# Expert weights moved as whole matrices, 16 KB in a row per partition, and activations turned by VectorE

## The chip, the cores and the metric

The kernel runs on one core of a Trainium2 chip. The metric is the device time of one launch in microseconds; the kernel before was timed in three runs.

## The reference

The program is a two-layer trunk on 256 tokens of 1024 numbers, all in float32. Layer 0 mixes tokens by causal pooling, layer 1 by differential attention; behind each mixer stands a mixture of 32 experts, of which every token uses two. The part that matters here is the expert block:

```
def expert_block(args):
    xb, e = args
    a = jax.nn.silu(xb @ w1[e]) * (xb @ w3[e])
    return a @ w2[e]
```

`w1` and `w3` are 1024x512 and `w2` is 512x1024, 2 MB each, so one expert is 6.3 MB of weights and the two layers together are 403 MB. About 16 tokens choose an expert on average.

## The kernel before

Nearly all that is read from memory are expert weights. They pass through `ring`, eight slots of 16 KB per partition (2 MB each). One slot holds one *chunk*, and an expert is three chunks (`CPE = 3`). Chunk 0 is the first half of the input rows of w1 and w3 together, chunk 1 the second half of both, chunk 2 is w2. SyncE issues every chunk as two transfers of 1 MB. In chunks 0 and 1 each partition gets 8 KB in a row from each matrix; in chunk 2 a partition reads four separate rows of w2, 4 KB each.

SyncE issues a chunk when its slot has been read: chunk `c` takes the slot of chunk `c-8`, and `used` says on what it waits. Slots with a first-half chunk come free at the semaphore `half`, those of a second-half chunk at `gu`, those of w2 at `y`. The eight first chunks of a layer are loaded ahead, in layer 1 behind the attention weights that stood in the slots.

TensorE works through the experts in groups of four (`E4`). For one expert (`expert(k)`) it does in this order: `gate_up` on chunk 0 and on chunk 1 (h times w1 and w3, 32 tokens a block, four column tiles of 32 side by side), `gather` of a quarter of the next group's tokens, a transpose of the activations `act`, and `down` on chunk 2. ScalarE and VectorE make silu(gate) * up between `gate_up` and the transpose, and VectorE copies the turned activations `actT` back from PSUM. After four experts `scatter` adds the results to their tokens. A second block of 32 tokens is skipped by a branch where an expert has at most 32 tokens.

```
used = (main["half"], main["gu"], main["y"])
...
sp.wait_ge(used[j], it * BODY + (layer * NE + e + 1))
load(c % RING, chunk_parts(layer, it * BODY + c // CPE, c % CPE), loaded[c % RING])
```

Of the kernel before, what the change touches and what calls it, by code (L numbers as in the profile page):

```python
# [18 lines left out]
ALU = mybir.AluOpType  # L19
ACT = mybir.ActivationFunctionType  # L20
# [73 lines left out]
def build(nc, x, norm_mix_g, norm_ffn_g, pool_w, pool_scale, wq, wk, wv, wo, lq1, lk1, lq2, lk2, subln_g,  # L94
          moe_wg, moe_bg, moe_we, moe_be, moe_w1, moe_w3, moe_w2, final_g, consts, out):
    with ExitStack() as ctx:
# [69 lines left out]
        at_ps = ps[:, 7, 0:256].rearrange("p (b r) -> p b r", b=NB)  # L166
# [39 lines left out]
        STEPS = ("onehot", "gated", "xg", "xgc", "half", "gu", "exp", "den", "sig", "gh", "act", "at", "atc", "y", "yc_v", "yc_a",  # L206
# [12 lines left out]
        def chunk_parts(layer, e, j):  # L219

            if j < 2:
                return [(m * 2048, w[layer, e, :, :].rearrange("(p k) n -> p k n", k=KT)[:, 4 * j:4 * j + 4, :])
                        for m, w in ((0, moe_w1), (1, moe_w3))]
            w = moe_w2[layer, e, :, :].rearrange("(j p) n -> p j n", p=P)
            return [(m * 2048, w[:, 2 * m:2 * m + 2, :]) for m in range(2)]

        def attn_parts(c):
            w = (wv, wq, wk, wo)[c // 2]
            if c < 6:
                w = w[0].rearrange("(p k) n -> p k n", k=KT)  # L230
            else:
                w = w[0].rearrange("(k p) n -> p k n", p=P)
            at = 4 * (c % 2)
            return [(m * 2048, w[:, at + 2 * m:at + 2 * m + 2, :]) for m in range(2)]

        def view(src):
            return src.shape[1], src.shape[2]
# [5 lines left out]
        def _(sp):  # L243
            def load(slot, parts, signal):
                for at, src in parts:
                    k, n = view(src)
                    sp.dma_start(ring[:, slot, at:at + k * n].rearrange("p (k n) -> p k n", k=k), src) \  # L247
                      .then_inc(signal, 16)
# [18 lines left out]
            used = (main["half"], main["gu"], main["y"])  # L267
# [65 lines left out]
        def _(pe):  # L333
# [72 lines left out]
            def group(s, g, u, placed, rounds, fullest, tokens, chunk):  # L406
# [9 lines left out]
                def expert(k):  # L416
# [4 lines left out]
                    for half in range(2):  # L421
                        w = ring[:, chunk(k, half), :].rearrange("p (m k n) -> p m k n", m=2, k=4)

                        def gate_up(b, qs, half=half, w=w):
                            for q in qs:
                                for j in range(JT):
                                    mm = pe.matmul(gu_ps[SB * j:SB * (j + 1), b, :, :], xg[:, u, 4 * half + q, b, k, :],  # L427
# [791 lines left out]
```

## Time and profile before

| | us |
|---|---|
| median of three runs (lowest, highest) | 1174.48 (1172.45, 1177.19) |
| the profiled execution's own time | 1172.21 |
| its span in the trace | 1170.4 |
| TensorE busy, VectorE busy, ScalarE busy | 888.4, 352.2, 216.5 |
| time of DMA packets of SyncE's queue, share of 16 engines' span | 88.8% |

The trace covers the span; another 1.8 us of the profiled execution's own time lie around it. Busy time of TensorE overstates its work, since matmuls are pipelined. The DMA share is the time of the packets themselves, summed over the sixteen DMA engines.

### The profile page before, as it was taken

The numbers are of one execution on the slowest core, as the hardware profiler recorded it, in microseconds if no ns is written. First come the engines' busy times: TensorE is split into PE (matmuls) and PEld (weight loads), VectorE is DVE, ScalarE is ACT, GpSimd is POOL, SyncE is SP. The second block draws the span as 40 slices with busy tenths as digits, with TensorE's granted clock in tenths as the row PEclk, the third lists the DMA queues.
The fourth block names the chain that finished last, engine by engine and source line by source line (L and its number), as shares of the span: only waits on it lengthen the run. The fifth ranks groups of instructions, "written<-read, shape, count | busy, mean of one in ns | idle before, by whom it ended". The sixth has DMA issues, their size and how long they took to land.

```text
span 1170.4 us, 20054 instructions
## 1 busy us (share of the span) xinstructions
PE 888.4 (76%) x8020; PEld 496.3 (42%) x8021; DVE 352.2 (30%) x814; ACT 216.5 (18%) x487; POOL 5.1 (0%) x15
## 2 busy tenths in 40 slices
PE   6878777766776677678999987898776757677765
PEld 4544434332433343333787554454433423334332
DVE  3523322221331222223156433222322312222223
ACT  3221212110111111111145312111111111112111
POOL 1000000000000000000000000000000000000000
PEclk9899979988998889899999989999998999888898
DMA  9979999999999999998503439999999999999992
GB/s 307 399 311 414 415 415 416 416 416 415 416 416 416 415 415 416 416 416 353 199 1 147 173 141 418 415 416 416 415 415 415 415 416 416 417 414 416 416 413 114
DMA packets 78121, 427.70 MB, mean 365 GB/s; under 512 B 7492, under 2 KB 8772, under 8 KB 43672
## 3 DMA queue, kind: packets, MB, share of 16 engines
q1 hardware_dynamic: 77528, 424.20, 88.8%
q8 instruction: 131, 2.15, 0.7%
q0 software_dynamic: 448, 1.25, 0.5%
q14 instruction: 14, 0.11, 0.0%
HBM read 424.37 MB, written 1.05 MB: 363 GB/s over the span
## 4 chain that ended last, share of the span: by engine, by line
SPq 41%; PE 30%; DMA 19%; DVE 5%; issue 4%; ACT 2%; DVEq 0%; ACTq 0%
SPq L247 40%; DMA ring<-in_moe_w 18%; PE ps L427 7%; PE ps L600 5%; PE ps L465 3%; PE ps L586 2%; PE ps L394 2%; PE ps L480 2%; PE ps L654 2%; DVE work L1024 1%; PE ps L379 1%; PE ps L346 1%; PE ps L561 1%; PE ps L374 1%; PE ps L338 1%
## 5 line engine op out<-in xcount | busy, mean ns | idle before, releaser
L427 PE MATMUL ps<-ring,work 128*32 128x256 f32 x4224 | 304.6, 437 | 178.7 <-DMA ring<-in_moe_w 123.9
L427 PEld LDWEIGHTS ps<-ring,work 128*32 128x32 f32 x4224 | 144.3, 123 | 331.3 <-DMA ring<-in_moe_w 151.2
L394 PE MATMUL ps<-work,h_sb 128*128 128x256 f32 x576 | 153.5, 412 | 7.1 <-ACT work L720 4.5
L1022 DVE TENSOR_SCALAR work<-work 128x128 f32<-128x128 f32 (+1 forms) x64 | 14.7, 230 | 476.5 <-ACT work L730 476.5
L465 PE MATMUL ps<-ring,work 128*32 128x256 f32 x2112 | 129.3, 386 | 25.7 <-DVE work L1051 25.5
L394 PEld LDWEIGHTS ps<-work,h_sb 128*128 128x128 f32 x576 | 110.2, 202 | 59.0 <-issue 38.6
L1054 DVE COPY hT<-ps 32x512 f32<-32x512 f32 x128 | 87.4, 683 | 139.5 <-PE ps L465 138.6
L730 ACT ACTIVATE work<-ps 128x256 f32<-128x256 f32 x64 | 24.6, 384 | 485.3 <-PE ps L427 485.3
L738 ACT COPY hT<-ps 32x512 f32<-32x512 f32 x128 | 74.1, 579 | 169.0 <-PE ps L465 168.3
L465 PEld LDWEIGHTS ps<-ring,work 128*32 128x32 f32 x2112 | 63.4, 110 | 75.6 <-DVE work L1051 32.7
L480 PE MATMUL ps<-hT,work 128*128 128x512 f32 x136 | 62.6, 604 | 11.1 <-DVE hT L1054 11.1
L720 ACT COPY work<-ps 128x512 f32<-128x512 f32 x72 | 42.2, 586 | 132.1 <-PE ps L394 126.7
L1024 DVE RECIPROCAL work<-work 128x128 f32<-128x128 f32 (+1 forms) x64 | 62.6, 978 | 2.2
L600 PE MATMUL ps<-hT,ring 128*128 128x256 f32 x256 | 56.5, 379 | 0.0
L600 PEld LDWEIGHTS ps<-hT,ring 128*128 128x128 f32 x256 | 48.2, 190 | 7.1 <-issue 0.5
L346 PE MATMUL ps<-cst,small 128*128 128x512 f32 x78 | 43.5, 645 | 3.5 <-issue 3.5
L480 PEld LDWEIGHTS ps<-hT,work 128*128 128x128 f32 x136 | 24.5, 189 | 49.2 <-issue 49.2
L447 PE MATMUL ps<-cst,work 128*128 128x128 f32 x64 | 20.7, 323 | 29.1 <-DVE work L1028 28.7
L1051 DVE COPY work<-ps 128x256 f32<-128x256 f32 x64 | 27.2, 425 | 50.0 <-PE ps L447 50.0
L447 PEld LDWEIGHTS ps<-cst,work 128*128 128x128 f32 x64 | 9.1, 142 | 56.7 <-issue 56.6
L654 PE MATMUL ps<-ring,work 128*128 128x512 f32 x64 | 28.6, 594 | 0.0
L586 PE MATMUL ps<-ring,hT 128*128 128x512 f32 x64 | 27.9, 594 | 0.8 <-DVE hT L918 0.8
(151 smaller groups left out, 454.9 us busy)
## 6 DMA issues: line engine op xcount, KB each, us to landing
ring<-in_moe_w SPq DMA_DIRECT2D x384, 1024.0 KB, 21.8
ring<-in_attn_wv SPq DMA_DIRECT2D x4, 1024.0 KB, 18.5
ring<-in_attn_wq SPq DMA_DIRECT2D x4, 1024.0 KB, 20.3
ring<-in_attn_wk SPq DMA_DIRECT2D x4, 1024.0 KB, 22.7
ring<-in_attn_wo SPq DMA_DIRECT2D x4, 1024.0 KB, 21.5
x_sb<-in_x SPq DMA_DIRECT2D x2, 512.0 KB, 6.3
work<-in_pool_w SPq DMA_DIRECT2D x1, 1024.0 KB, 12.9
out_x<-h_sb SPq DMA_DIRECT2D x2, 512.0 KB, 2.7
```

The source lines that it names most:

```text
L247: sp.dma_start(ring[:, slot, at:at + k * n].rearrange("p (k n) -> p k n", k=k), src) \
L346: pe.matmul(ps[:, bank, :], zero, cst[:, 0:512], start=True, stop=True)
L394: mm = pe.matmul(xg_ps[:, q, :], h_sb[:, t, kt * P:(kt + 1) * P], onehot[:, u, t].rearrange("p b e s -> p (b e s)"), start=(t == 0), stop= ...
L427: mm = pe.matmul(gu_ps[SB * j:SB * (j + 1), b, :, :], xg[:, u, 4 * half + q, b, k, :], w[:, :, q, P * j:P * (j + 1)], start=(half == 0 and ...
L465: mm = pe.matmul(y_ps[SB * i:SB * (i + 1), b, :], actT[:, b, SB * j:SB * (j + 1)], w[:, j, 256 * i:256 * (i + 1)], start=(j == 0 and b == ...
L480: mm = pe.matmul(acc[:, t, i, :], gateT[:, b, t * P:(t + 1) * P], y[:, b, 512 * i:512 * (i + 1)], start=False, stop=False, skip_group_chec ...
L586: mm = pe.matmul(ps[:, 2 * t + i, :], hT[:, kt, t * P:(t + 1) * P], matrix(0, kt)[:, 512 * i:512 * (i + 1)], start=(kt == 0), stop=(kt == ...
L600: mm = pe.matmul(ps[:, h % 2, i * S:(i + 1) * S], matrix(2 + 2 * i, kt)[:, h * P:(h + 1) * P], hT[:, kt, :], start=(kt == 0), stop=(kt == ...
L654: mm = pe.matmul(ps[:, 2 * t + i, :], qT[:, h, t * P:(t + 1) * P], matrix(6, h)[:, 512 * i:512 * (i + 1)], start=(h == 0), stop=(h == NH - 1))
L738: ins = act_e.copy(y[SB * k:SB * (k + 1), :, 256 * i:256 * (i + 1)], y_ps[SB * i:SB * (i + 1), :, :])
L1024: ve.reciprocal(sg[:, 2, b, :], sg[:, 1, b, :]).then_inc(s["sig"], 1)
L1054: ins = ve.tensor_copy(y[SB * k:SB * (k + 1), :, 256 * i:256 * (i + 1)], y_ps[SB * i:SB * (i + 1), :, :])
```

## The change

Each chunk is now one whole matrix: chunk 0 is w1, chunk 1 is w3, chunk 2 is w2. It is moved in one transfer of 2 MB, in which each partition reads one run of 16 KB. For w2 this needs another order of its 512 input rows: partition p holds rows 4p to 4p+3. The activations have to stand in that order, and `ve.transpose`, which turns 32x32 blocks, writes them so from `act` to `actT` in SBUF; the transpose on TensorE and VectorE's copy out of PSUM are gone, and so is the semaphore `half`.

`gate_up` of an expert now needs chunks 0 and 1 both from its first matmul on, and both slots come free at `gu`. Where the two lie in slots 7 and 0 the order of gate and up in PSUM is swapped (`swapped`, `gates`). The attention weights are moved in one transfer per chunk as well.

```diff
             if j < 2:
-                return [(m * 2048, w[layer, e, :, :].rearrange("(p k) n -> p k n", k=KT)[:, 4 * j:4 * j + 4, :])
-                        for m, w in ((0, moe_w1), (1, moe_w3))]
-            w = moe_w2[layer, e, :, :].rearrange("(j p) n -> p j n", p=P)
-            return [(m * 2048, w[:, 2 * m:2 * m + 2, :]) for m in range(2)]
+                return (moe_w1, moe_w3)[j][layer, e, :, :].rearrange("(p k) n -> p (k n)", k=KT)
+            return moe_w2[layer, e, :, :].rearrange("(p j) n -> p (j n)", j=JT)
...
-            def load(slot, parts, signal):
-                for at, src in parts:
-                    k, n = view(src)
-                    sp.dma_start(ring[:, slot, at:at + k * n].rearrange("p (k n) -> p k n", k=k), src) \
-                      .then_inc(signal, 16)
+            def load(slot, src, signal):
+                dst = ring[:, slot, :]
+                if len(src.shape) == 3:
+                    dst = dst.rearrange("p (k n) -> p k n", k=src.shape[1])
+                sp.dma_start(dst, src).then_inc(signal, 16)
...
-            used = (main["half"], main["gu"], main["y"])
+            used = (main["gu"], main["gu"], main["y"])
...
-                        gate_up(0, range(0, 3))
-                        second_block(count, lambda: gate_up(1, range(0, 4)))
-                        gate_up(0, range(3, 4)).then_inc(s["half"] if half == 0 else s["gu"], 1)
+                    lo, hi = sorted((chunk(k, 0), chunk(k, 1)))
+                    w = ring[:, lo:hi + 1:hi - lo, :].rearrange("p m (k n) -> p m k n", k=KT)
...
+                    gate_up(0, range(0, 4))
+                    second_block(count, lambda: gate_up(1, range(0, 4)))
+                    gate_up(0, range(4, 7))
+                    second_block(count, lambda: gate_up(1, range(4, 8)))
+                    gate_up(0, range(7, 8)).then_inc(s["gu"], 1)
...
-                    pe.wait_ge(s["act"], n1)
-                    second_block(count, lambda: pe.transpose(at_ps[:, 1, :], act[:, 1, :], ident))
-                    pe.transpose(at_ps[:, 0, :], act[:, 0, :], ident).then_inc(s["at"], 1)
...
-                    pe.wait_ge(s["atc"], n1)
+                    pe.wait_ge(s["actT"], n1)
...
+                ve.wait_ge(s["act"], n1)
+
+                for i in range(blocks):
+                    ins = ve.transpose(actT[:, i, :].rearrange("p (q s) -> p q s", q=JT),
+                                       act[:, i, :].rearrange("p (i q) -> p q i", q=JT))
+                ins.then_inc(s["actT"], 1)
...
-                    ve.wait_ge(s["at"], n1)
-                    ve.tensor_copy(actT[:, :, :], at_ps).then_inc(s["atc"], 1)
```

**TensorE, the first expert of a group, from its first gate_up matmul on.** The rows give the line, the operation, what it writes and reads, and the semaphores it waits for (`loaded0` is the landing of slot 0). Before:

```order
L427 MATMUL ps<-ring,work 32x256 [waits loaded0]
L427 MATMUL ps<-ring,work 32x256 x11
L413 COMPARE_AND_BRANCH
L427 MATMUL ps<-ring,work 32x256 x16
L413 UNCONDITIONAL_BRANCH
L427 MATMUL ps<-ring,work 32x256 x4
L427 MATMUL ps<-ring,work 32x256 [waits loaded1]
L427 MATMUL ps<-ring,work 32x256 x11
L413 COMPARE_AND_BRANCH
```

The same place in the changed kernel:

```order
L423 MATMUL ps<-ring,work 32x256 [waits loaded1,loaded0]
L423 MATMUL ps<-ring,work 32x256 x15
L409 COMPARE_AND_BRANCH
L423 MATMUL ps<-ring,work 32x256 x16
L409 UNCONDITIONAL_BRANCH
L423 MATMUL ps<-ring,work 32x256 x12
L409 COMPARE_AND_BRANCH
```

The wait for the second chunk has moved ahead of all matmuls of the expert.

**SyncE, the first loads of the loop that refills the ring.** `m_half`, `m_gu` and `m_y` are the semaphores of `used`. Before:

```order
L247 ISA [waits m_half]
L247 DMA ring<-in_moe_w 128x2x1024
L247 ISA
L247 DMA ring<-in_moe_w 128x2x1024
L247 ISA [waits m_gu]
L247 DMA ring<-in_moe_w 128x2048 x2
L247 ISA [waits m_y]
```

In the changed kernel:

```order
L244 ISA [waits m_gu]
L244 DMA ring<-in_moe_w 128x4096
L244 ISA [waits m_gu]
L244 DMA ring<-in_moe_w 128x4096
L244 DMA ring<-in_moe_w 128x4096 [waits m_y]
```

The first load of a layer's refill has moved from the half-way point of the first expert's gate_up to its end, and each chunk is one transfer in place of two.

**VectorE, one expert with one block, from the second multiplication on.** Before:

```order
L1028 TENSOR_TENSOR work<-work,ps 128x128 [waits m_gh]
L1048 UNCONDITIONAL_BRANCH
L1050 REGISTER_ALU
L1051 COPY work<-ps 128x256 [waits m_at]
L1054 COPY hT<-ps 32x2x256 [waits m_y]
```

In the changed kernel:

```order
L1023 TENSOR_TENSOR work<-work,ps 128x128 [waits m_gh]
L1027 STREAM_TRANSPOSE work<-work 128x128 [waits m_act]
L1049 UNCONDITIONAL_BRANCH
L1051 REGISTER_ALU
L1053 COPY hT<-ps 32x2x256 [waits m_y]
```

The copy that waited for TensorE's transpose is gone, and a transpose that waits only for VectorE itself stands in its place.

## Rows read from the trace of the kernel before

**Rows 1.** The page: span, rate in 40 slices, packets.
```profile
span 1170.4 us, 20054 instructions
...
GB/s 307 399 311 414 415 415 416 416 416 415 416 416 416 415 415 416 416 416 353 199 1 147 173 141 418 415 416 416 415 415 415 415 416 416 417 414 416 416 413 114
DMA packets 78121, 427.70 MB, mean 365 GB/s; under 512 B 7492, under 2 KB 8772, under 8 KB 43672
```

**Rows 2.** The page: the DMA queues, then the expert weights' transfers.
```profile
q1 hardware_dynamic: 77528, 424.20, 88.8%
q8 instruction: 131, 2.15, 0.7%
...
ring<-in_moe_w SPq DMA_DIRECT2D x384, 1024.0 KB, 21.8
```

**Rows 3.** The chain that ended last, by engine.
```profile
SPq 41%; PE 30%; DMA 19%; DVE 5%; issue 4%; ACT 2%; DVEq 0%; ACTq 0%
```

**Rows 4.** Windows over the two refills; columns by engine, then PEclk, DMA share, GB/s.
```profile
66.00:514.00 448.00, 321.49 (x3339) 166.80 (x3338) 119.94 (x245) 70.53 (x132) 0.00 (x0) 0.91 1.02 416
...
703.00:1148.00 445.00, 327.95 (x3533) 173.74 (x3533) 120.43 (x241) 69.69 (x130) 0.00 (x0) 0.92 1.01 412
```

**Rows 5.** TensorE's waits, 130 to 500 us: total, times, longest.
```profile
PE ps L427 <- DMA ring<-in_moe_w: 50.9, 25, 3.1
PE ps L427 <- issue: 32.5, 18, 3.5
```

**Rows 6.** The DMA view, 716 to 720 us, while w2 is moved.
```profile
DMA packets 410, 1.63 MB, mean 409 GB/s; under 512 B 18, under 2 KB 18, under 8 KB 405
...
q1 hardware_dynamic: 409, 1.62, 101.2%
```

**Rows 7.** The same view, 706 to 714 us, while w1 and w3 are moved.
```profile
DMA packets 462, 3.39 MB, mean 423 GB/s; under 512 B 47, under 2 KB 47, under 8 KB 52
...
q1 hardware_dynamic: 461, 3.37, 100.6%
```

**Rows 8.** Windows late in the loads of layers 0 and 1.
```profile
548.00:556.00 8.00, 8.00 (x22) 3.69 (x21) 2.72 (x9) 1.25 (x3) 0.00 (x0) 1.00 0.51 209
...
1142.00:1148.00 6.00, 1.93 (x32) 0.94 (x32) 0.00 (x0) 0.00 (x0) 0.00 (x0) 1.00 0.50 207
```

**Rows 9.** Timeline, layer 0's first expert: start, duration, instruction.
```profile
62.16 3.66 PE L427 MATMUL ps<-ring,work 128*32 128x256 f32 x64 [0.77 <-ACT work L720]
...
64.31 76.94 SPq L247 DMA_DIRECT2D ring<-in_moe_w  x37
...
65.88 0.38 ACT L730 ACTIVATE work<-ps 128x256 f32<-128x256 f32 x1 [3.87 <-PE ps L427]
```

**Rows 10.** Timeline, layer 1's first expert.
```profile
698.47 33.14 SPq L247 DMA_DIRECT2D ring<-in_moe_w  x20
...
700.38 1.59 PEld L394 LDWEIGHTS ps<-work,h_sb 128*128 128x128 f32 x8 [0.41 <-issue]
```

**Rows 11.** Timeline, layer 0's last expert, second chunk.
```profile
514.60 1.93 PE L427 MATMUL ps<-ring,work 128*32 128x256 f32 x32 [3.09 <-DMA ring<-in_moe_w]
```

**Rows 12.** Timeline, layer 1's last expert.
```profile
1148.68 3.35 PE L427 MATMUL ps<-ring,work 128*32 128x256 f32 x32 [4.38 <-DMA ring<-in_moe_w]
...
1152.79 0.95 DVE L1024 RECIPROCAL work<-work 128x128 f32<-128x128 f32 x1
...
1154.10 0.29 DVE L1028 TENSOR_TENSOR work<-work,ps 128x128 f32<-128x128 f32 x1
...
1155.54 1.93 PE L465 MATMUL ps<-ring,work 128*32 128x256 f32 x32 [0.52 <-DVE work L1051]
```

**Rows 13.** Timeline, one gate_up at a lower clock.
```profile
285.77 2.79 PE L427 MATMUL ps<-ring,work 128*32 128x256 f32 x24 [3.48 <-issue]
...
290.62 4.44 PE L427 MATMUL ps<-ring,work 128*32 128x256 f32 x40 [2.06 <-issue]
```

**Rows 14.** Windows, the clock in that stretch.
```profile
288.00:292.00 4.00, 1.94 (x24) 0.69 (x20) 0.00 (x0) 0.00 (x0) 0.00 (x0) 0.50 1.01 416
```

More of the change, by code:

```diff
@@ L229, in attn_parts @@
             if c < 6:
[L230 to L237, printed above, removed]
+                return w[0].rearrange("(p k) n -> p (k n)", k=KT)[:, CH * (c % 2):CH * (c % 2 + 1)]
+            return w[0].rearrange("(k p) n -> p k n", p=P)[:, 4 * (c % 2):4 * (c % 2) + 4, :]
         block = ctx.enter_context(nc.Block())
@@ L420, in expert, with gate_up @@
                         pe.wait_ge(s["xgc"], rounds)
[L421 to L427, printed above, removed]
-                                                   w[:, :, q, P * j:P * (j + 1)],
-                                                   start=(half == 0 and q == 0 and b == 0),
-                                                   stop=(half == 1 and q == 3), skip_group_check=True)
-                            return mm
-                        gate_up(0, range(0, 3))
-                        second_block(count, lambda: gate_up(1, range(0, 4)))
-                        gate_up(0, range(3, 4)).then_inc(s["half"] if half == 0 else s["gu"], 1)
+                    lo, hi = sorted((chunk(k, 0), chunk(k, 1)))
+                    w = ring[:, lo:hi + 1:hi - lo, :].rearrange("p m (k n) -> p m k n", k=KT)
+                    def gate_up(b, kts):
+                        for kt in kts:
+                            for j in range(JT):
+                                mm = pe.matmul(gu_ps[SB * j:SB * (j + 1), b, :, :], xg[:, u, kt, b, k, :],
+                                               w[:, :, kt, P * j:P * (j + 1)], start=(kt == 0 and b == 0),
+                                               stop=(kt == KT - 1), skip_group_check=True)
+                        return mm
+                    gate_up(0, range(0, 4))
[3 more added lines that the diff above has]
+                    gate_up(0, range(7, 8)).then_inc(s["gu"], 1)
                     if k == 0:
@@ L747, in experts @@
                         group(main, it * GPB + (layer * NGRP + gg), gg % 2,
-                              it * (GPB * E4) + (layer * (NGRP + 1) + gg + 1) * E4)
+                              it * (GPB * E4) + (layer * (NGRP + 1) + gg + 1) * E4,
+                              lambda k, gg=gg: int(swapped(gg * E4 + k)))
                 fb = more[layer]
```

40 lines of the change are left out of this document (21 added, 19 removed).

## The prediction

> **What bounds the kernel now.** Read the rate before the engines' busy time. Of forty slices 29 stand at 413 to 418 GB/s, and a long hole lies between them, where layer 1's attention runs [rows 1]. So there are two long stretches in which memory traffic sets the pace, one for each layer's experts, and the rest is paced by other things. The DMA engines' share is 1.01 to 1.02 in both stretches, with TensorE at a mean granted clock of 0.91 and 0.92 and busy for 72% and 74% of them [rows 4]. TensorE waits for weights inside its stretch: 25 waits of up to 3.1 us between 130 and 500 us, 50.9 us in all [rows 5].
>
> The chain of waits must be read with care. It gives 41% to SyncE's queue [rows 3], which looks like an issue cost. But an issue counts there as long as the full queue holds SyncE back, and a transfer lands 21.8 us after its issue [rows 2]. At 416 GB/s that is 9.1 MB, or 4.3 of the ring's eight chunks under way. SyncE is late for nothing; the DMA engines are full.
>
> A refill starts when the first slot is freed and ends for TensorE when the last expert's second chunk has landed: 64.31 to 514.60 us in layer 0 and 698.47 to 1148.68 us in layer 1 [rows 9 to 12]. Both last 450.2 to 450.3 us, for chunks 8 to 94, which are 87 chunks or 29 experts. That is 15.53 us an expert, where 6.29 MB at 416 GB/s would take 15.12. The difference is seen late in each layer's loads: the share is 0.51 and 0.50, at 209 and 207 GB/s [rows 8], so half of the engines is done and the other half still has a backlog. The queue of instruction packets has 131 packets and 0.7% of 16 engines' span [rows 2], 131 us or 1.0 us each; if they fall to one half, they account for 8 us of its lag per layer. The change leaves the code's length nearly as it is, and I keep this lag.
>
> **Fewer and longer packets.** Here lies the gain. An engine serves 8 of the 128 partitions. An expert costs it 8 x (4 + 4) = 64 data packets now (four of 8 KB and four of 4 KB per partition) and 8 x 3 = 24 of 16 KB after: 40 fewer for the same bytes. What a packet costs beside its bytes is bounded from two views. In throughput: while w2 is moved in 4 KB rows the rate is 409 GB/s, while w1 and w3 are moved in 8 KB rows it is 423 [rows 6, 7]. A chunk of 2.097 MB takes 5.13 us at the first rate. The mean over an expert, 15.12, then leaves 5.00 for each of the others. With 16 fewer packets per engine that is 0.13/16 = 8 ns a packet. In packet time: 101.2% of 16 x 4 us over 391 data packets is 166 ns for 4 KB; 100.6% of 16 x 8 us, less five short packets, over 409 is 313 ns for 8 KB. Twice the first less the second is 19 ns. No row shows a 16 KB packet of data. I take 12 ns, nearer to the lower value, since throughput is what counts and packets overlap a little (a share over 1.0). That gives 40 x 12 = 0.48 us an expert, 29 x 0.48 = 13.9 us a layer, **-27.8 us** for both. The ends are -18.6 (8 ns) and -44 (19 ns). Half as many transfers also means half as many completion packets; their cost is inside these shares, and I add nothing.
>
> The Trainium skill speaks for less ("DMA: Bandwidth & Descriptors", Why small descriptors are slow): it states about 3 cycles of overhead per packet, and elsewhere on the page a fabric clock of 850 MHz, so 3.5 ns. By that estimate 40 packets would be worth 0.14 us an expert and the two refills 8 us. The trace shows more than twice that between 4 and 8 KB; what lies above 8 KB no row here tells.
>
> **Slots are freed later.** The first load of a refill waited for half a gate_up and now waits for the whole. In layer 0 the load was issued at 64.31 and gate_up ends at 62.16 + 3.66 = 65.82 [rows 9]: +1.5 us. In layer 1 it was issued at 698.47, and the gather behind gate_up starts at 700.38 [rows 10]: +1.9. Nothing hides this, because the ring is full then and the DMA engines are idle. **+3.4 us**. Two slots now come free at once, 9.8 us of work, so the next release (`y`, 5.4 us behind `gu` in the expert that ran from 1148.68 [rows 12]) is in time. Inside the refill the late release costs nothing: at worst three slots hold landed chunks and five are under way, 24 us of work, and even the half that is ahead by some 12 us has a backlog.
>
> **The last expert starts from nothing.** While chunk 0 landed first, half of gate_up was done before chunk 1 came. Now all 64 matmuls of it wait for chunk 1. Before, 32 matmuls stood behind the last landing: 1.93 us in layer 0 and 3.35 us in layer 1 [rows 11, 12]. Now 64 do: 3.66 us at full clock [rows 9], 2.79 + 4.44 = 7.23 us as seen at the lower level [rows 13], where the granted clock was 0.50, so 1.2 GHz [rows 14]. TensorE will have stood still before each expert for some 6 us (worked out with the third rival), and I take 5.5 us, between the ends: +3.6 and +2.2, **+5.8 us** (ends +2.0 and +9.2). The w2 chunk lands some 5 us behind chunk 1 and is there by then. After that everything is as before: layer 0's end starts the attention, whose weights land at the pace at which they did.
>
> **Turning the activations.** From the end of VectorE's last product at 1154.39 to the first `down` matmul at 1155.54 pass 1.15 us [rows 12]: a handover, a transpose, a handover, a copy, and 0.52 us of handover. What stays is one VectorE instruction on 128x128 and the 0.52. The transpose isn't in the trace; the product took 0.29 us and the reciprocal of the same shape 0.95, so it is 0.8 to 1.5 us in all. It moves as many elements as the product: I take 0.85, so -0.3 us at each layer's end, **-0.6 us** (ends -0.7 and +0.7). For the other 62 experts it lies under the wait for weights. The swap of gate and up changes addresses only. Merging the attention weights' transfers is worth nothing: they land under the attention's own work, and the ring refills in the gaps.
>
> **Sum**: -27.8 + 3.4 + 5.8 - 0.6 = -19.2 us. From the profiled execution's 1172.21 that gives 1153.0; it lies 2.3 us under the median of the runs, 1174.48, so the prediction is 1155. With all terms at their fast ends it is -39 us, with all at their slow ends -5, so this case's own range is 1135 to 1169.
>
> **Rivals.**
>
> *Packets above 8 KB bring nothing.* Then only w2 gains, 0.13 us an expert, 58 x 0.13 = -7.5, against +8.6 of the other terms: 1175.6, no change. For it: the longest data packets seen are 8 KB. Against it: 128 of 8 KB still cost something over their bytes by both views. The skill's 3 cycles per packet, quoted above, lead to nearly the same time. Chance 0.10.
>
> *The late start and the late end alone.* If 409 against 423 GB/s comes from where w2's rows lie and not from the packets, the refill runs as before and +8.6 remains: 1183, slower. It happens at the first and the last expert of each layer, and decides as soon as an expert gains under 8.6/58 = 0.15 us. Against it: 4 and 8 KB stretches follow each other by the chunk. Chance 0.06.
>
> *TensorE becomes the bound.* Its work for an expert is now in one piece, and then it stands still, 15.0 - (3.66 + 3.5 + 1.93) = 6 us, with 3.5 us from gate_up's end to `down` and 1.93 for `down` [rows 12]. If that lets the clock fall and it stays at 1.2 GHz, an expert takes 7.2 us for gate_up, at least 3.5 for the gather and the activations, 3.9 for `down` and 32.5/24 = 1.4 of waits marked as issue [rows 5], 16.0 us before scatter is counted. It decides from 15.0 on: at 16.0 the refills are 58 x 0.47 = 27 us longer than now and the kernel takes 1174.5 + 27 + 8.6 = 1210. For it: at 285 us a gate_up took twice as long at granted clock 0.50 [rows 13, 14]. The skill ("TensorE: Matmul & The Clock Gate", What's actually happening) says that the low clock is the default and activity lifts it, which speaks for longer stretches at 1.2 GHz here. Against it: a TensorE that is late has no gap any more, and the mean clock stays at 0.91 to 0.92 here although waits of up to 3.1 us occur [rows 4, 5]. Chance 0.05.
>
> **How the numbers follow.** The likeliest case has 0.79; 0.02 of it falls within 0.5% of the time before. Five microseconds either way, some 0.5%, is about what three runs can tell from no change. Faster 0.77; same 0.12 (the first rival and that 0.02); slower 0.11. The range 1140 to 1176 holds most of the likeliest case and the first rival.
>
> **What would show it.** Right: the refills run at 425 to 430 GB/s, no data packet below 16 KB in them, and from first refill issue to the last second chunk 436 us in place of 450; first issues 1.5 and 1.9 us later against the start of gate_up; 64 matmuls behind the last landing; a mean granted clock near 0.8. Wrong: 8 KB packets in the table, a rate still at 416, or a rate that dips because SyncE waits for `gu` while the DMA share is below 1.

## The result, and the profile after

The changed kernel takes 1167.45 us (median of 6 runs, 1163.12 to 1168.44), the kernel before 1174.57 us beside it. The ratio is 0.993, with a 95% interval of 0.9905 to 0.9954. It is faster by 7 us; 19 were forecast. The profiled execution of the changed kernel took 1163.12 us and its span is 1161.3 us, 9.1 us less than the span of [rows 1]. The traces explain these 9.1 us; 2 of them are the luck of which executions were profiled.

The page of the changed kernel, the lines that answer to [rows 1 to 3], and the group of the new transpose:

```profile
span 1161.3 us, 19468 instructions
...
GB/s 308 404 286 426 426 422 425 426 426 424 424 426 426 424 424 427 425 426 308 184 1 150 170 116 404 427 426 424 426 426 426 423 424 427 426 423 424 427 400 98
DMA packets 33196, 427.74 MB, mean 368 GB/s; under 512 B 4292, under 2 KB 5572, under 8 KB 7704
...
q1 hardware_dynamic: 32600, 424.18, 86.7%
q8 instruction: 134, 2.20, 0.8%
...
PE 43%; DMA 39%; DVE 8%; issue 6%; ACT 2%; DVEq 0%; SPq 0%; ACTq 0%
...
L1027 DVE STREAM_TRANSPOSE work<-work 128x128 f32<-128x128 f32 x66 | 26.5, 404 | 2.2
...
ring<-in_moe_w SPq DMA_DIRECT2D x192, 2048.0 KB, 29.5
```

The rate of the two plateaus rose from 416 to about 425 GB/s with the same bytes in fewer than half the packets. SyncE's 41% of the chain is gone and stands under DMA now, although nothing about the bound has changed. What has changed is where SyncE stands still. It waits 612 us in all for slots that gate_up frees, where it waited 128 us before. That is why a share of the chain is no price.

Windows over the two refills and late in each layer's loads (columns as in [rows 4]), which answer to [rows 4] and [rows 8]:

```profile
66.00:508.00 442.00, 311.09 (x3276) 171.37 (x3274) 119.24 (x245) 70.47 (x132) 0.00 (x0) 0.91 1.00 424
700.00:1128.00 428.00, 316.96 (x3408) 173.22 (x3404) 116.41 (x235) 67.57 (x126) 0.00 (x0) 0.89 1.01 425
544.00:548.00 4.00, 4.00 (x10) 1.71 (x9) 2.22 (x9) 0.79 (x2) 0.00 (x0) 1.00 0.53 212
1132.00:1136.00 4.00, 1.49 (x28) 0.65 (x20) 1.37 (x2) 1.16 (x2) 0.00 (x0) 1.00 0.49 205
```

The DMA share is still 1.00 and 1.01, so the DMA engines are the bound as before. The half of them that lags at the end is still there (0.53 and 0.49).

The DMA view of 130 to 480 us:

```profile
DMA packets 10208, 148.68 MB, mean 425 GB/s; under 512 B 1133, under 2 KB 1133, under 8 KB 1133
...
q1 hardware_dynamic: 10160, 147.90, 99.7%
```

As many packets are under 8 KB as are under 512 B. The other 9027 of SyncE's queue carry 147.90 MB, which is 16.4 KB each, so all weights go in 16 KB packets.

The timeline at the first expert of layer 0, the first and the last of layer 1, and the last of layer 0, which answers to [rows 9 to 12]:

```profile
62.11 3.66 PE L423 MATMUL ps<-ring,work 128*32 128x256 f32 x64 [0.88 <-ACT work L714]
...
65.99 0.89 SPq L244 DMA_DIRECT2D ring<-in_moe_w  x2
...
508.18 3.66 PE L423 MATMUL ps<-ring,work 128*32 128x256 f32 x64 [3.40 <-DMA ring<-in_moe_w]
...
692.66 3.66 PE L423 MATMUL ps<-ring,work 128*32 128x256 f32 x64 [0.88 <-ACT work L714]
...
696.55 0.89 SPq L244 DMA_DIRECT2D ring<-in_moe_w  x2
...
1138.02 5.13 PE L423 MATMUL ps<-ring,work 128*32 128x256 f32 x64 [4.53 <-DMA ring<-in_moe_w]
...
1145.52 0.41 DVE L1027 STREAM_TRANSPOSE work<-work 128x128 f32<-128x128 f32 x1
1145.98 1.93 PE L459 MATMUL ps<-ring,work 128*32 128x256 f32 x32
```

These points and those of [rows 9 to 12] cut each span into five pieces, whose differences give the whole 9.1 us:

| piece | before | after | difference |
|---|---|---|---|
| start to layer 0's first issue | 64.31 | 65.99 | +1.7 |
| refill of layer 0, to the last expert's second chunk | 450.29 | 442.19 | -8.1 |
| from there to layer 1's first issue | 183.87 | 188.37 | +4.5 |
| refill of layer 1 | 450.21 | 441.47 | -8.7 |
| from there to the end | 21.72 | 23.28 | +1.6 |

### The profile page after: what moved, and what is told of

It is laid out like the page before. It is cut to its first block, busy times and chain, and to the rows that moved or that the text cites. A ratio compares the mean times of both kernels' runs of the same rounds, so it can differ in the third digit from the quotient of the medians.

```text
span 1161.3 us, 19468 instructions
## 1 busy us (share of the span) xinstructions
PE 876.3 (75%) x7954; PEld 507.3 (44%) x7955; DVE 351.3 (30%) x816; ACT 216.5 (19%) x487; POOL 5.1 (0%) x15
## 4 chain that ended last, share of the span: by engine, by line
PE 43%; DMA 39%; DVE 8%; issue 6%; ACT 2%; DVEq 0%; SPq 0%; ACTq 0%
DMA ring<-in_moe_w 39%; PE ps L423 15%; PE ps L459 6%; PE ps L594 5%; PE ps L474 3%; PE ps L390 3%; DVE work L1019 2%; PE ps L580 2%; PE ps L648 2%; DVE work L1027 1%; ACT work L724 1%; PE ps L375 1%; ACT work L714 1%; DVE work L1021 1%; DVE work L1023 1%
## 5 line engine op out<-in xcount | busy, mean ns | idle before, releaser
L423 PE MATMUL ps<-ring,work 128*32 128x256 f32 x4224 | 316.7, 453 | 195.9 <-DMA ring<-in_moe_w 120.7
L423 PEld LDWEIGHTS ps<-ring,work 128*32 128x32 f32 x4224 | 169.9, 129 | 334.3 <-issue 247.7
L459 PE MATMUL ps<-ring,work 128*32 128x256 f32 x2112 | 128.7, 385 | 33.1 <-DVE work L1027 32.4
L390 PE MATMUL ps<-work,h_sb 128*128 128x256 f32 x576 | 145.6, 396 | 5.2 <-ACT work L714 4.5
L390 PEld LDWEIGHTS ps<-work,h_sb 128*128 128x128 f32 x576 | 104.8, 192 | 57.2 <-issue 38.6
L459 PEld LDWEIGHTS ps<-ring,work 128*32 128x32 f32 x2112 | 62.8, 110 | 97.2 <-DVE work L1027 48.2
L474 PEld LDWEIGHTS ps<-hT,work 128*128 128x128 f32 x136 | 24.5, 189 | 50.3 <-issue 50.3
L1027 DVE STREAM_TRANSPOSE work<-work 128x128 f32<-128x128 f32 x66 | 26.5, 404 | 2.2
L342 PEld LDWEIGHTS ps<-cst,small 128*128 128x128 f32 x78 | 13.7, 195 | 14.5 <-issue 13.6
L1021 DVE TENSOR_TENSOR work<-work,ps 128x128 f32<-128x128 f32 (+1 forms) x64 | 18.6, 291 | 2.2
```

The source lines that it names most:

```text
L342: pe.matmul(ps[:, bank, :], zero, cst[:, 0:512], start=True, stop=True)
L390: mm = pe.matmul(xg_ps[:, q, :], h_sb[:, t, kt * P:(kt + 1) * P], onehot[:, u, t].rearrange("p b e s -> p (b e s)"), start=(t == 0), stop= ...
L459: mm = pe.matmul(y_ps[SB * i:SB * (i + 1), b, :], actT[:, b, SB * j:SB * (j + 1)], w[:, j, 256 * i:256 * (i + 1)], start=(j == 0 and b == ...
L474: mm = pe.matmul(acc[:, t, i, :], gateT[:, b, t * P:(t + 1) * P], y[:, b, 512 * i:512 * (i + 1)], start=False, stop=False, skip_group_chec ...
```

## The experiments

The forecast rests on one price, what a packet costs beside its bytes, and on 8.6 us given back at the ends of the layers. The experiments vary the packets at an unchanged program, the release of the slots, and the turn of the activations. "Refill" is the piece of the table above, for layer 0 and layer 1, and a rate is that of 130 to 480 us. Packets are data packets per DMA engine and expert.

**The changed kernel with shorter packets** (`e1_two_8k`, `e2_two_2x4k`). Each chunk is again two transfers: halves of each row (8 KB), or every second 4 KB.

```diff
-                sp.dma_start(dst, src).then_inc(signal, 16)
+                for m in range(2):
+                    ...
+                        half = src[:, 2048 * m:2048 * (m + 1)]
+                    sp.dma_start(dst, half).then_inc(signal, 16)
```

> The changed kernel, but each chunk in two transfers with 8 KB per partition in a row (48 data packets per engine and expert in place of 24; waits, slots and TensorE's order unchanged). Theory A, a packet costs about 9 ns beside its bytes at every length: 24 x 9 ns = 0.21 us more an expert, refills at about 420 GB/s in place of 425, each refill 6 us longer, the kernel 12 us slower than the changed one, so about 1179. Theory B, above 8 KB there is nothing to gain because another limit holds: same rate and time as the changed kernel, 1167.

> The changed kernel, but each chunk in two transfers of every other 4 KB piece (96 data packets per engine and expert in place of 24). Theory A: 72 x 9 ns = 0.65 us more an expert, refills at about 408 GB/s, the kernel 36 us slower than the changed one, about 1204. Theory B (a cost only below 8 KB, of 0.13 us per matrix): 3 x 0.13 x 58 = 23 us slower than the changed one, about 1190.

Measured: 1179.09 us, ratio 1.0044 [1.0025, 1.0063], and 1202.03 us, ratio 1.0244 [1.0221, 1.0267]. The DMA view of 130 to 480 us of the first:

```profile
DMA packets 20072, 146.58 MB, mean 419 GB/s; under 512 B 2226, under 2 KB 2226, under 8 KB 2226
...
q1 hardware_dynamic: 20026, 145.83, 100.4%
```

and of the second:

```profile
DMA packets 36630, 141.79 MB, mean 405 GB/s; under 512 B 2150, under 2 KB 2150, under 8 KB 36585
...
q1 hardware_dynamic: 36585, 141.05, 101.5%
```

Refills: 448.88 and 447.21 us with 48 packets, 461.34 and 459.26 us with 96, against 442.19 and 441.47 with 24. So 24 packets more cost 12.4 us in 58 experts, 12.4/(58 x 24) = 8.9 ns each; the next 48 cost 24.5 us, 8.8 ns each. The price is the same above 8 KB as below it. The first rival, by which packets above 8 KB bring nothing, falls. The share suggests how 19 ns came about: it is over 100% at 4 and 8 KB (101.5%, 100.4%), so packets overlap there, and 99.7% at 16 KB. Packet time then overstates what a packet takes from the throughput.

**The chunks of before, w2 in longer packets** (`e3_halves`, `e8_w2_one_16k`). w1 and w3 are moved in halves as before, with the early semaphore; w2 has the new order and the turn is VectorE's. w2 goes in two transfers of 8 KB rows, or in one of 16 KB rows.

```diff
-            w = moe_w2[layer, e, :, :].rearrange("(j p) n -> p j n", p=P)
+            w = moe_w2[layer, e, :, :].rearrange("(p j) n -> p j n", j=JT)
             return [(m * 2048, w[:, 2 * m:2 * m + 2, :]) for m in range(2)]
```

> The kernel before with its half chunks and early releases, only with VectorE's transpose and w2 in 8 KB rows (48 data packets per engine and expert, as in the run with two 8 KB transfers; 64 before). Theory A plus the priced start and end: 16 x 9 ns x 58 = 8.4 us off the refills and 1.3 us off the turns at the two layer ends, none of the 3.4 us of late start and 3.5 us of late end: about 1165, 14 us faster than the run with two 8 KB transfers of whole matrices less 1 us of noise. Rival C, the late release also starves the DMA engines inside the refills of the changed kernel (slots held too long): then the refill here runs at a higher rate than in the run with two 8 KB transfers of whole matrices, although the packets are the same.

> The kernel before with VectorE's transpose and w2 in one transfer with 16 KB rows; w1 and w3 stay in half chunks of 8 KB rows that are freed early. 40 data packets per engine and expert (64 before, 48 in the run with halves, 24 in the changed kernel). Theory A: 24 x 8 ns x 58 = 11 us off the refills, 1.3 us off the ends, no late start and no late end: about 1164, at or below the changed kernel. Rival, by the run with halves (half the expected gain in its refills): about 1168, no better than the changed kernel.

Measured: 1170.10 us, ratio 0.9961 [0.9947, 0.9975], refills 448.84 and 448.37; and 1167.85 us, ratio 0.9938 [0.9915, 0.9961], refills 446.43 and 445.82. The first has 48 packets, like `e1_two_8k`, the same rate of 419 GB/s and the same refill in layer 0 (448.84 against 448.88), and yet is 9.0 us faster. That is the price of chunks that are whole matrices, at the ends of the layers. The second, with 40 packets and the early release, is as fast as the changed kernel with 24. Both are 4 to 5 us slower than expected; the runs on TensorE's program below show a cause for most of it. Against `e7_turn_only` (64 packets, refills 452.66 and 452.41) the first gives 8.2 and 8.7 ns a packet. The step from the first to the second is only eight packets and gives 10.4 and 11.0 ns.

**Slots freed later still** (`e6_release_at_y`). The slots of w1 and w3 come free only at the end of `down`.

```diff
-            used = (main["gu"], main["gu"], main["y"])
+            used = (main["y"], main["y"], main["y"])
```

> The changed kernel, but all three slots of an expert are freed only at y, behind down (two of them some 5 us later than at gu). Theory A: inside a refill the queue of transfers is deep enough, so the refill keeps 442 us and 425 GB/s, and only its start is 5 us later in each layer: 10 us slower than the changed kernel, about 1177. Rival C, late releases also starve the DMA engines inside the refill: the rate falls below 425 and the time goes beyond 1185.

Measured: 1176.54 us, ratio 1.0014 [0.9998, 1.0031], 9.1 us over the changed kernel. Its timeline at layer 0's first refill:

```profile
62.88 3.66 PE L423 MATMUL ps<-ring,work 128*32 128x256 f32 x64 [0.88 <-ACT work L714]
...
71.52 1.36 SPq L244 DMA_DIRECT2D ring<-in_moe_w  x3
```

The first issue stands 8.64 us behind the start of gate_up in place of 3.88, 4.8 us more per layer, 9.5 for both. The refills are 442.24 and 440.66 us, no longer than those of the changed kernel. A late release costs its own delay once per layer, where the ring is full and the DMA engines are idle, and nothing inside the refill.

**Gate and up in two passes** (`e4_two_passes`). w1's products come first and free their slot, then w3's: twice as many matmuls, of half the width.

```diff
+                    for m in range(2):
+                        w = ring[:, chunk(k, m), :].rearrange("p (k n) -> p k n", k=KT)
...
+                        gate_up(0, range(7, 8)).then_inc(s["half"] if m == 0 else s["gu"], 1)
...
-            used = (main["gu"], main["gu"], main["y"])
+            used = (main["half"], main["gu"], main["y"])
```

> The changed kernel with whole matrices in 16 KB rows, but gate_up in two passes: w1 as soon as chunk 0 is there, w3 after chunk 1, 128 columns a matmul instead of 256, and the slot of w1 freed after the first pass. Theory A: refills as in the changed kernel (442 us), first issue about 1.7 us earlier, less of gate_up behind the last landing (1.8 to 2.5 us less a layer): 7 to 8 us faster than the changed kernel, about 1160. Rival D, twice as many matmuls of half the width cost TensorE more than they free (weight loads set their pace): a pass takes as long as the joined gate_up, the start and the end gain nothing and the time is 1167 or more. Rival C: the refills get faster too, by up to 6 us each.

Measured: 1325.91 us, ratio 1.1283 [1.1245, 1.1321], where 1160 had been expected. TensorE's waits from 130 to 500 us, then the window of 130 to 480 us, then the page's queue of instruction packets:

```profile
PE ps L423 <- issue: 93.8, 37, 5.4
```

```profile
130.00:480.00 350.00, 231.87 (x3417) 155.40 (x3413) 77.65 (x160) 45.50 (x85) 0.00 (x0) 0.84 0.90 363
```

```profile
q8 instruction: 198, 3.24, 1.0%
```

The DMA share fell to 0.90: this kernel is no longer bound by memory. TensorE stands for 93.8 us for nothing that the profile shows, and 198 instruction packets are fetched in place of 134. Which of the two costs the time, the doubled matmuls or the code that they take, this run doesn't separate. Whole matrices can't be released early in this way.

**No second block** (`e5_no_second_block`). The changed kernel without the branches for a second block of 32 tokens; the tokens above 32 of an expert are left out of the computation.

```diff
                     if count is None:
                         step()
-                    else:
-                        with pe.If(count > SB):
-                            step()
```

> The changed kernel without TensorE's code for a second block of 32 tokens (the products of the tokens above 32 in the two experts that have them are left out; for all other experts that code is only jumped over). Theory A, the half of the DMA engines that finishes late is late because it also moves instruction packets: fewer of them than 134 (about 90), the refills' excess over bytes divided by rate falls from 12 to 13 us to about 9, each refill about 3 us shorter; TensorE's waits marked issue fall too. Time about 1160. Rival: the lag has another cause and the refills stay at 442 us; then 1165 to 1167.

Measured: 1154.68 us, ratio 0.9835 [0.9808, 0.9861], 12.8 us under the changed kernel. The page's queue:

```profile
q8 instruction: 86, 1.41, 0.5%
```

48 instruction packets fewer, and refills of 436.75 and 437.17 us: 5.4 and 4.3 us shorter, at 426 GB/s and with the same data packets. Where they come from is seen at the end of layer 1's loads, in windows of 4 us, first in the changed kernel (the window from 1132 us is shown above), then here:

```profile
1128.00:1132.00 4.00, 3.10 (x32) 1.92 (x27) 2.16 (x5) 0.97 (x2) 0.00 (x0) 1.00 0.62 262
...
1136.00:1140.00 4.00, 1.98 (x20) 1.13 (x24) 0.00 (x0) 0.00 (x0) 0.00 (x0) 0.70 0.47 197
1140.00:1144.00 4.00, 4.00 (x52) 2.41 (x45) 0.34 (x2) 0.38 (x1) 0.00 (x0) 0.87 0.11 41
```

```profile
1122.00:1126.00 4.00, 1.93 (x32) 0.94 (x32) 1.88 (x4) 1.67 (x3) 0.00 (x0) 1.00 0.67 287
1126.00:1130.00 4.00, 1.83 (x31) 1.33 (x35) 0.18 (x1) 0.00 (x0) 0.00 (x0) 0.93 0.47 201
1130.00:1134.00 4.00, 4.00 (x43) 2.48 (x36) 0.01 (x1) 0.38 (x1) 0.00 (x0) 0.64 0.12 49
```

There are four windows with a share below 1 in the changed kernel (0.62, 0.49, 0.47, 0.11) and three here (0.67, 0.47, 0.12): the half of the DMA engines that lags is some 4 us less behind, which is what this refill gained. The branches, which are hardly ever taken, cost the two refills about 10 us. That some computation is gone too is no likely reason, since the DMA share is 1.00 over both refills here as well.

The number of instruction packets explains only a part. Each refill has 23 fewer (58 and 57 in the changed kernel, 35 and 34 here, by the DMA view of 66 to 500 and 700 to 1125 us). At 1.0 to 1.1 us each, over the half of the engines that lags, these are some 3 us, an estimate from those rows; 5.4 and 4.3 were measured. The rest can lie in where TensorE's remaining code now stands, which the runs with TensorE's program kept show to be worth 1.7 and 2.6 us.

**Only the turn, only the order of w2** (`e7_turn_only`, `e9_order_only`, `e10_turn_alone`). All three move what the kernel before moves, in 64 data packets. `e9_order_only` takes w2's rows in another order and keeps TensorE's transpose; `e10_turn_alone` takes VectorE's transpose and keeps w2's order; `e7_turn_only` has both, w2 in pieces of 4 KB. In all three the activations meet other rows of w2 than in the reference, so the product differs.

The first cut is of `e9_order_only` (also in `e7_turn_only`), the second of `e10_turn_alone` and `e7_turn_only`, where VectorE's transpose is put in as in the change.

```diff
-            w = moe_w2[layer, e, :, :].rearrange("(j p) n -> p j n", p=P)
-            return [(m * 2048, w[:, 2 * m:2 * m + 2, :]) for m in range(2)]
+            w = moe_w2[layer, e, :, :].rearrange("(p k m) n -> p k m n", k=2, m=2)
+            return [(m * 2048, w[:, :, m, :]) for m in range(2)]
```

```diff
-                    pe.wait_ge(s["act"], n1)
-                    second_block(count, lambda: pe.transpose(at_ps[:, 1, :], act[:, 1, :], ident))
-                    pe.transpose(at_ps[:, 0, :], act[:, 0, :], ident).then_inc(s["at"], 1)
...
-                    ve.wait_ge(s["at"], n1)
-                    ve.tensor_copy(actT[:, :, :], at_ps).then_inc(s["atc"], 1)
```

> The kernel before with VectorE's transpose and w2 in the order that it needs, but still two transfers of two 4 KB pieces, so the packets (64 per engine and expert), slots and releases are those of before. Theory A: 0.67 us less at each layer's end, nothing else: 1 to 2 us faster than before, about 1173.5. Rival: the transpose on TensorE and its copy also cost inside the refills, then it is 4 us or more faster.

> The kernel before, TensorE's transpose kept, but w2's 4 KB pieces are read in another order: each transfer gives a partition two pieces out of one 16 KB run (pitch 16 KB between partitions) instead of two rows that lie beside those of its neighbours. The product of w2 is formed with its rows in another order than the activations. Packets stay at 64 per engine and expert. Theory E, the old row order of w2 was the cheaper one in memory: refills 3 us longer each, about 5 to 6 us slower than before, 1180. Rival F, the order costs nothing and the refills of the run with the turn alone were longer because of VectorE's transposes or the changed code: no change, 1175.

> The kernel before with its own loads of w2, only the turn is made by VectorE; w2's rows keep the old order, so that its product differs. Theory E: 1.3 us less at the two layer ends, refills 450 us as before: about 1173.5. Rival F: refills 3 us longer each, 1179 as in the run with the turn and the new order of 4 KB pieces.

Measured: 1179.06 us, ratio 1.0036 [1.002, 1.0052]; 1175.91 us, 1.0013 [0.9996, 1.003]; 1178.34 us, 1.0043 [1.0028, 1.0057]. The order costs nothing that can be told. The turn makes the kernel slower by 5 us, and the refills of `e10_turn_alone` are 452.64 and 452.73 us, 2.4 and 2.5 longer than before at the same packets. The prediction has no term for that. Nor does this run gain at the ends of the layers: from gate_up's end to `down` pass 3.71 and 3.66 us, where 3.50 and 3.51 passed before. `down` stands there behind TensorE's own gather, which took 2.98 us in layer 0 in place of 1.99.

**Is it VectorE's transpose?** (`f1_turn_twice`, `f2_copy_for_turn`). On top of `e10_turn_alone` the transpose is done twice, or a plain copy stands in its place (nothing is turned then). In the expectations of these and the following runs, cause G is VectorE's new instruction and cause H the shift of TensorE's program, from which instructions were taken out.

```diff
-                    ins = ve.transpose(actT[:, i, :].rearrange("p (q s) -> p q s", q=JT),
-                                       act[:, i, :].rearrange("p (i q) -> p q i", q=JT))
+                    ins = ve.tensor_copy(actT[:, i, :], act[:, i, :])
```

> The run with the turn alone (kernel before, VectorE's transpose, old order of w2), but VectorE turns every block twice, once into a scratch tile. Cause G: the refills get another 3 us longer each, about 1184. Cause H: TensorE's program is unchanged, refills 452 to 453 us and about 1178, at most 1 us more at the layer ends.

> The run with the turn alone, but VectorE copies the activations in place of turning them (down works on activations that are not turned). Same number of instructions on every engine. Cause G, if it is the transpose as such: refills back at 450 us, about 1173. Cause H: 452 to 453 us and 1178.

Measured: 1180.24 us, ratio 1.0055 [1.0033, 1.0076], refills 452.82 and 452.45; and 1178.35 us, ratio 1.0043 [1.003, 1.0056], refills 452.60 and 452.42. Neither doubling nor removing the transpose moves the refill, so it isn't the cause.

**Or TensorE's program?** (`f3_turn_pe_code_kept`, `f5_changed_pe_code_kept`). TensorE keeps its transposes where they were and nobody waits for them; VectorE's transpose feeds `down`. Once this stands on `e10_turn_alone` (w2's order as there, product differs), once on the changed kernel.

```diff
+                    pe.wait_ge(s["act"], n1)
+                    second_block(count, lambda: pe.transpose(at_ps[:, 1, :], act[:, 1, :], ident))
+                    pe.transpose(at_ps[:, 0, :], act[:, 0, :], ident).then_inc(s["at"], 1)
```

> The run with the turn alone, but TensorE's transposes stay in its program and write a PSUM bank that nobody reads, so that TensorE's code is as long as before. Cause H: refills 450 us and no instruction packet over 1.3 us, about 1174. Cause G: 452 to 453 us and 1178 or more.

> The changed kernel with TensorE's transposes kept in its program as idle code (they write a PSUM bank that nobody reads). Cause H, the shift of TensorE's code costs each refill 2 to 3 us: refills 439 us in place of 442, about 1162, 5 us faster than the changed kernel. If the shift does nothing here: 1167.

Measured: 1171.41 us, ratio 0.9987 [0.9975, 0.9999], refills 450.21 and 448.65; and 1163.49 us, ratio 0.9906 [0.9885, 0.9926], refills 440.46 and 438.89. Work that nobody needs makes each kernel faster, the one by 6.9 us and the other by 4.0; their refills are together 6.5 and 4.3 us shorter. One place where it shows is TensorE's waits in layer 1's refill (710 to 1130 us), whose "issue" waits at gate_up are, in `e10_turn_alone` and then in `f3_turn_pe_code_kept`:

```profile
PE ps L427 <- issue: 33.4, 15, 4.9
```

```profile
PE ps L427 <- issue: 11.9, 6, 3.6
```

The kernel before has this row in the same stretch, and the changed kernel this one:

```profile
PE ps L427 <- issue: 13.4, 8, 3.5
```

```profile
PE ps L423 <- issue: 31.2, 15, 5.3
```

With TensorE's old program the longest such wait in this stretch is 3.5 or 3.6 us, without it 4.9 or 5.3, whatever the data packets are. The total is no measure of the loss: from 130 to 500 us it is 29.4 us in the changed kernel and 29.7 in `f5_changed_pe_code_kept`. The page counts 131 instruction packets in the first case and 134 in the second.

The trace shows what lies in these waits. Every one of TensorE's "issue" waits of over 2 us between 70 and 1140 us (11 in the kernel before, 15 in the changed kernel, 13 in `f5_changed_pe_code_kept`) begins within 1.3 us of the start of an instruction packet. In the changed kernel's five longest, of 4.8 to 5.3 us, two instruction packets start within 0.8 us of each other, and one of them takes 2.0 to 2.3 us. In the other two kernels no two start so close in the refills and none takes over 1.2 us. One of these waits in the changed kernel, with the instruction packets of 279 to 282 us:

```profile
284.93 3.28 PE L423 MATMUL ps<-ring,work 128*32 128x256 f32 x32 [5.06 <-issue]
```

```profile
q8 instruction: 2, 0.03, 7.2%
```

The same place of the kernel before is the 3.48 us in [rows 13], with these from 282 to 285 us:

```profile
q8 instruction: 1, 0.02, 2.3%
```

These long waits recur after some 121 us, which are eight experts, one trip of TensorE's loop.

The lag at the end of layer 1's loads depends on TensorE's program too, by the DMA share. In windows of 1 us it is near a half from 1129 to 1141 us in the changed kernel and from 1129 to 1139 us in `f5_changed_pe_code_kept`, whose windows of 4 us are:

```profile
1126.00:1130.00 4.00, 3.27 (x37) 2.11 (x39) 2.16 (x5) 0.72 (x2) 0.00 (x0) 1.00 0.83 348
1130.00:1134.00 4.00, 0.53 (x12) 0.05 (x4) 1.37 (x2) 1.16 (x2) 0.00 (x0) 1.00 0.50 213
1134.00:1138.00 4.00, 2.95 (x28) 1.61 (x32) 0.00 (x0) 0.00 (x0) 0.00 (x0) 0.50 0.51 213
1138.00:1142.00 4.00, 4.00 (x42) 2.23 (x35) 0.00 (x0) 0.38 (x1) 0.00 (x0) 0.65 0.10 41
```

So it is shown that the change to TensorE's program causes the loss, and that instruction packets fall together with it. That the pairs are what makes a refill longer is only argued: `e5_no_second_block` has the same pairs and waits of up to 5.4 us, and yet the shortest refills, with 23 instruction packets fewer in each. The kept transposes are also work, not only code. A better clock is not how they help, since from 130 to 480 us it is 0.87 with them and 0.90 without, and that refill is 1.7 us shorter all the same; but no run keeps the length of the program without the work.

The Trainium skill ("Runtime: NRT & Kernel Launch", Instruction fetch mechanics) says that an engine's instruction memory is refilled in blocks of 16 KiB by the sequencer's own DMA queue, and that the cost of crossing into the next block is mostly hidden. The trace agrees on the size: 2.15 MB in 131 packets are 16.4 KB each. The cost is not hidden here at the places named above: the waits that begin with one or two of these packets last up to 5.3 us.

**A version with the best of each** (`e11_mixed`, `f4_mixed_pe_code_kept`). Of every eight experts the first and the last are moved in halves, with the early release and the split gate_up of before, and the other six as whole matrices; w2 is one transfer everywhere. `f4_mixed_pe_code_kept` also keeps TensorE's transposes.

```diff
+        def by_halves(e):
+            return e % BODY in (0, BODY - 1)
...
+            if j < 2 and halves:
+                return [w[layer, e, :, :].rearrange("(p k) n -> p (k n)", k=KT)[:, 2048 * j:2048 * (j + 1)]
+                        for w in (moe_w1, moe_w3)]
```

> The changed kernel, but of every eight experts the first and the last keep w1 and w3 in half chunks of 8 KB rows that are used and freed one after the other; the other six move whole matrices. It should keep most of the gain in the refills and lose neither the start nor the end: first issue 2.2 us behind the first gate_up (3.9 in the changed kernel), 32 matmuls behind the last landing in place of 64 (1.7 us less each), against 16 x 9.8 ns for each of 14 to 15 experts, 2.3 us. 4 to 5 us faster than the changed kernel, about 1163. Rival: the late start and end of the changed kernel cost nothing that the halves give back, then it is 2 us slower than the changed kernel, 1169.

> The mixed kernel (first and last of eight experts in half chunks, the others as whole matrices) with TensorE's transposes kept as idle code. Cause H: refills about 3 us shorter each, 1155. Cause G: no gain, 1160 to 1161.

Measured: 1159.98 us, ratio 0.9881 [0.9857, 0.9906], refills 443.96 and 441.95; and 1154.84 us, ratio 0.9839 [0.9816, 0.9862], refills 441.14 and 440.01. The end of layer 1 in the second, whose last landing again has 32 matmuls behind it:

```profile
1128.82 1.91 PE L451 MATMUL ps<-ring,work 128*32 128x256 f32 x32
...
1133.73 3.35 PE L451 MATMUL ps<-ring,work 128*32 128x256 f32 x32 [2.99 <-DMA ring<-in_moe_w]
```

Its first issue stands 2.16 us behind the start of gate_up, as before. The late first load and the 64 matmuls behind the last landing are both avoided, and it is 18 us faster than the kernel before and some 12 us faster than the changed one.

## Why the prediction was right in its direction and wrong in its size

**What bounds the kernel.** Right (the plateaus are 30 of the 40 slices, not 29). The DMA share is 1.00 to 1.01 in both refills, and their rate rose as the packets fell. SyncE's 41% of the chain went without a gain of its own.

**Fewer and longer packets**: -27.8 forecast, -16.8 measured over both refills. This is the step that failed, and it failed in its price: "I take 12 ns" between bounds of 8 and 19. With TensorE's transposes kept in both kernels (`f3_turn_pe_code_kept` to `f5_changed_pe_code_kept`) 40 packets fewer are worth 9.75 and 9.76 us a layer, 19.5/(58 x 40) = 8.4 ns; the shorter packets give 8.9 and 8.8 ns. The lower bound was the right one, since it came from throughput, though with some luck: taken straight from 409 and 423 GB/s in place of the mean of 416, the same windows would have given 2.097 MB x (1/409 - 1/423), or 0.17 us for 16 packets, 10.6 ns. The other took packet time for throughput, although shares over 1.0 stood in [rows 6, 7] and said that packets overlap. At 8.4 ns the term is -19.5. The estimate of 3.5 ns that the prediction made from the Trainium skill's 3 cycles ("DMA: Bandwidth & Descriptors", Why small descriptors are slow) is too low here by a factor of 2.4.

**What the refills lost.** The rest is the term that the prediction lacked. "The change leaves the code's length nearly as it is" was the wrong sentence: 1.7 and 2.6 us a layer were lost to TensorE's changed program (440.46 and 438.89 with the old one, 442.19 and 441.47 without). Nor was the lag kept: at the end of layer 1 the share is near a half for 12 us in place of 10. Against this stands a small gain that I can't name: with the old program and the faster turn the refills are 0.1 and 1.6 us shorter than before. Together -1.7 - 19.5 + 4.3 = -16.9.

**Slots are freed later**: +3.4 forecast. The first issue is 3.88 and 3.89 us behind the start of gate_up in place of 2.15 and 2.17: +3.4. `e6_release_at_y` shows that a further delay adds itself and nothing else, as the prediction said of the inside of the refill.

**The last expert starts from nothing**: +5.8 forecast, 3.66 and 5.13 in place of 1.93 and 3.35 measured: +3.5. The mechanism was right. The size wasn't, since layer 0's last gate_up ran at the full clock, 3.66 us after a wait of 3.40 us, and layer 1's took 5.13. 5.5 us had been taken for both. That was no bad price: in other kernels with the same end this gate_up took 5.08 and 6.09 us (`e1_two_8k`) and 5.19 and 6.48 (`f5_changed_pe_code_kept`), and 3.66 again in layer 0 of `e6_release_at_y`. The comparison of `e1_two_8k` with `e3_halves` puts the late start and the late end together at 9.0 us, against 9.2 forecast.

**Turning the activations**: -0.6 forecast, -1.4 measured. From the end of gate_up to `down` pass 2.83 us in both layers, where 3.50 and 3.51 passed before. The transpose takes 0.40 us, about half of the 0.85 assumed.

**As before in the attention**: not quite. Of the +4.5 us between the refills the last gate_up has 1.7 and the late issue 1.7, and the turn takes 0.7 off; +1.7 remains: from layer 0's last `down` to layer 1's first gate_up pass 176.27 us before and 177.99 after. This stretch varies that much without the change. In `e9_order_only`, which loads the attention weights as the kernel before does, it is 178.86 us, and in `e3_halves`, which does too, 176.83. So the 1.7 us are no evidence that the merged transfers of the attention weights cost anything.

**The sum.** -16.8 + 3.4 + 3.5 - 1.4 + 1.7 and 0.5 behind the last `down` give -9.1, the difference of the spans. All three rivals are refuted. Each step of packet length pays; the late start and end don't stand alone, since `e1_two_8k` and `e2_two_2x4k` change the packets at the same places in memory and the refills follow; and the DMA share stays at 1.00 with a mean granted clock of 0.89 to 0.91 in the refills. The mean clock near 0.8 was wrong too: it is about 0.9 although TensorE waits up to 6.2 us before a gate_up.

```profile
PE ps L423 <- DMA ring<-in_moe_w: 61.8, 18, 6.2
```

This row of TensorE's waits (130 to 500 us, changed kernel) stands beside 3.1 us in [rows 5]: the wait for a whole expert has come together in one piece, as the change makes it, and costs nothing inside the refill.

## What to carry to other kernels

When memory traffic is the bound, count packets per DMA engine, price them from the throughput of two stretches that differ in packet length, and don't price them from packet time where the share goes over 1.0. Long rows pay by the packet in every expert, while the coarse chunk costs once per layer at its first release and its last landing; so keep the fine chunks where a layer begins and ends and use the coarse ones between. Before an edit that takes instructions out of an engine's loop is booked as free, compare the number of instruction packets, whether two of them come together, and the longest "issue" waits: a few instructions more or less were worth 4 to 7 us here.

## What the runs showed of the hardware that was not expected

A data packet costs 8 to 9 ns beside its bytes, at 4 KB, 8 KB and 16 KB alike (8.2 to 9.0 over steps of 16 packets and more): 405, 419 and 425 GB/s in one program with 96, 48 and 24 data packets per engine and expert.

A program with 48 instruction packets fewer (86 in place of 134) had refills that were 5.4 and 4.3 us shorter, with the same data packets. Twice as many matmuls, with 198 instruction packets, left TensorE waiting for 93.8 us of 370 and made the kernel 13% slower, with memory at 363 GB/s.

Transposes on TensorE whose result nobody reads made two kernels 4.0 and 6.9 us faster. With them, one instruction packet came at a time in the refills and TensorE's waits there ended after at most 3.8 us; without them, two came together once in eight experts and the longest waits lasted 4.7 to 5.3 us.

VectorE's transpose of 128x128 float32 in 32x32 blocks takes 0.40 us on the page of the changed kernel.
